# Two transformer blocks on one core: probabilities of the second block's attention turned by VectorE and DRAM instead of TensorE

## The chip, the cores and the metric

The kernel runs on one core of one Trainium2 chip. The metric is device time in microseconds (us). Three timed runs of the kernel before gave 1270.28, 1270.36 and 1270.67; their median is 1270.36.

## The reference

512 tokens of width 1024 in fp32 pass through two blocks. The first is a hybrid layer (a short convolution, stick-breaking attention, a state-space mixer and block attention, gated and merged, then a feed-forward layer). The second, in which the change lies, is this:

```python
h = rmsnorm_2(x, norm_g)
q, k, v, za, u, vs, zs, gm = jnp.split(h @ w_in, IN_SPLITS_2, axis=-1)
q = partial_rope(q.reshape(B, S, 16, 64), pos)     # 16 query heads of 64
k = partial_rope(k.reshape(B, S, 2, 64), pos)      # 2 key/value heads
a = window_sink_attention(q, k, v, att_sinks)      # below
a = (a * silu(za)) @ w_att_out
sgo = chunked_spatial_gating(gelu(u), gelu(vs), sg_w, sg_b, ln_g, ln_b)  # layer norm of vs, mixing weights sg_w
sgo = (sgo * silu(zs)) @ w_sg_out
ga, gs = jnp.split(sigmoid(gm + b_merge), 2, axis=-1)
x = rmsnorm_2(x + (ga * a + gs * sgo) @ w_o, final_g)

# window_sink_attention: chunks of 64 queries see their own chunk and the two before
s = einsum('bnqhgd,bnkhd->bhgnqk', qc, kb) * 64 ** -0.5
m = maximum(max(s), sink)
p = exp(s - m)
o = einsum('bhgnqk,bnkhd->bnqhgd', p / (sum(p) + exp(sink - m)), vb)
```

The value product sums over keys, so the probabilities, which come out of the softmax with a query in each partition, have to be turned until a key stands in each partition.

## The kernel before

**Matrix products.** A product with fp32 accuracy is made of three passes. Each weight tile that lands in `raw` is split in two: ScalarE makes the high part `whi` (`split`, line 1491), GpSimd the low part `wlo` as the rest (`rest`, lines 789 to 793). The activations stand in SBUF as `hh` and `hl`. TensorE then runs `whi` on `hh`, `whi` on `hl` and `wlo` on `hh` into one PSUM bank (`gemm_fm`, lines 961 to 969; `wide_unit`, lines 985 to 991, with tokens as the stationary side). Weights, high parts and low parts have two slots each. A unit is 256 columns of weights (1 MB); SyncE loads one when GpSimd has finished with its slot (`slot_free`), ScalarE splits it once TensorE has finished with the slot of its high part.

**The attention of the second block** is spread over these products. It has 32 steps s: 8 pairs of heads m, each with 4 token tiles c of 128 tokens. Two steps are a batch v (16 batches). The work of a batch is put into slots, small gaps that hooks open inside the products: in units of q and za after the k-th multiplication (table `W_AT`, six slots in a pair of units), then one slot behind each token tile of the four wide units (16 slots), then the rest at the first unit of the attention's output product. The same counter i runs over the slots on every engine:

- TensorE, `w_slot` (line 1360): in an even slot i the scores of batch i/2 (`w_scores`, line 1332) and the value products of steps i-4 and i-3 (`w_values`, line 1355); in every slot the transposes of step i-2 (`w_turn`, line 1343). The first token tile of a head pair sees 128 keys of its own only and takes two transposes and two value products; the other tiles see 256 and take four of each.
- VectorE: in an even slot the maximum over the scores (`w_soft`), then, after ScalarE's exponentials, the sums and the multiplication by the reciprocal (`w_norm`, lines 2690 to 2696). Once per head pair it multiplies the attention's output by the gate (`w_out`, semaphore `w_o`).
- ScalarE: exponentials in an even slot (`w_exp`, lines 1839 and 1843), and in each slot the copy of the turned tile from PSUM to `wpt` (`w_turned`, line 1852). Between them it makes the high parts of the weights.

The semaphores: `w_ps` scores made, `w_nm` maximum made, `w_read` and `w_e` exponentials made, `w_p` probabilities made (`wp`, three buffers by step), `w_t` transposed, `w_pt` copied to `wpt`, `w_v` value products made.

**SyncE's queue** is a program written in order: weights of each unit, the swapped rows of the rotary embedding (`swap_rotary`), and the rows of x, which VectorE turns in blocks of 32 x 32 (line 2758) and SyncE stores to DRAM in four pieces (`store_turned`, line 718). A wait in it holds back everything behind it.

**The first block's attention** already turns its probabilities so: VectorE in blocks of 32 x 32, SyncE stores `p_blocks` to `p_rows` in four pieces and loads them back as `p_t` (`turned_through`, lines 628 to 639).

Of the kernel before, what the change touches and what calls it, by code (L numbers as in the profile page):

```python
# [29 lines left out]
P = 128  # L30
KD = DM // P
TT = SEQ // P
# [61 lines left out]
def build_program(nc, par_xt, cst1, cst2a, w_in, w_branch, w_o, w_gu, w_down, w_in2, sg_w, sg_b, ln_g,  # L94
# [8 lines left out]
    with ctx:  # L103
# [122 lines left out]
        wpt = place("wpt", [P, 2, SEQ], Z0 + 92)  # L226
        att_t = place("att_t", [P, SEQ], Z0 + 96)
# [94 lines left out]
        STEPS = KD * TT  # L322

# [46 lines left out]
        xs_rows = nc.dram_tensor("xs_rows", (SEQ, BW), f32, kind="Internal").ap()  # L370
        p_rows = nc.dram_tensor("p_rows", (2, P, 1280), f32, kind="Internal").ap()
# [180 lines left out]
        def _(sp):  # L552
# [75 lines left out]
            def turned_through(i):  # L628

                sp.wait_ge(sem("p_turned"), i + 1)  # L630
                for f in range(4):
                    sp.dma_start(p_rows[i % 2].rearrange("(j a) (k c) -> a k j c", a=32, c=P)[:, :, :, 32 * f:32 * f + 32],
                                 p_blocks[32 * f:32 * f + 32, :].rearrange("a (k j b) -> a k j b", j=4, b=32)).then_inc(sem("p_stored"), 16)
                if 2 <= i < HEADS + 2:
                    sp.wait_ge(sem("mo_o"), i - 1)
                elif i >= HEADS + 2:
                    sp.wait_ge(sem("st_o"), i - HEADS - 1)
                sp.wait_ge(sem("p_stored"), 64 * (i + 1))
# [22 lines left out]
            for f, (n0, part, h0) in enumerate(ffn_units):  # L661
# [21 lines left out]
                sp.dma_start(lng[:, :], ln_g.partition_broadcast(P)).then_inc(sem("c2_in"), 16)  # L683
                stream(n0 + part + 2, 2, down_from(2 * UC))
                sp.wait_ge(sem("tile_free"), tiles_before(n0 + part))
                sp.dma_start(lnb[:, :], ln_b.partition_broadcast(P)).then_inc(sem("c2_in"), 16)
                sp.dma_start(bsb[:, :, :].rearrange("p g i -> p (g i)"), sg_b.partition_broadcast(P)).then_inc(sem("c2_in"), 16)
# [33 lines left out]
            for p in range(4):  # L721
                for j, c0 in enumerate((I2_Q, I2_ZA)):
                    n = n_qz + 2 * p + j
                    slot_free(n)
                    load(n, cols(w_in2, c0 + p * UC, UC))
                    if p == 0 and j == 1:
                        sp.wait_ge(sem("key_s"), 1)
                        for a, b in ((0, 8), (8, 0)):
                            for kv in range(2):
                                sp.dma_start(key_t[a:a + 8, kv, :], key_s[64 * kv + b:64 * kv + b + 8, :]).then_inc(sem("key_in"), 16)  # L730
# [2363 lines left out]
```

## Time and profile before

| | |
|---|---|
| median of three runs | 1270.36 us |
| the profiled execution | 1270.71 us |
| its span, first to last instruction | 1268.9 us |
| mean granted clock of TensorE | 0.999 |
| TensorE busy | 1261.5 us |
| VectorE busy | 893.3 us |
| GpSimd busy | 724.1 us |
| ScalarE busy | 619.7 us |

How to read it: the trace holds one execution, whose own time stands beside its span; what lies between the two, 1.8 us, is outside the recorded instructions. Busy times of an engine are sums over its instructions. Matmuls are pipelined: one starts before the last has ended, so the distance from start to start tells what an instruction adds to the stream, not its duration. Times in the rows below are us from the start of the span.

### The profile page before, as it was taken

To read this page: it belongs to the slowest core of one execution; us is meant where nothing else is said; L and a number is where in the kernel's file an instruction comes from. 1 tells how busy PE (TensorE), PEld (TensorE's weight loads), DVE (VectorE), ACT (ScalarE), POOL (GpSimd) and SP (SyncE) were. 2 spreads that over 40 slices of the span, in tenths; PEclk is the share of its full clock that TensorE was granted. 3 is DMA by queue.
4 is the path that set the end of the run, shared out by engine and by line. 5 is a ranking of instruction groups with operands and counts; after the bars stand their busy time and mean duration, and the time that the engine had idled before them with its cause. 6 is when DMAs were issued, how large, how long until landed. Compare 5 with 4: busy or idle time off the path is not lost.

```text
span 1268.9 us, 19753 instructions
## 1 busy us (share of the span) xinstructions
PE 1261.5 (99%) x7542; PEld 1091.2 (86%) x7542; DVE 893.3 (70%) x1380; ACT 619.7 (49%) x989; POOL 724.1 (57%) x513
## 2 busy tenths in 40 slices
PE   9999999999999999999999999999999999999998
PEld 7877877777888899989988998877778899999886
DVE  6775555777444599558855869766656999998587
ACT  6123533565334555325522546354556656666454
POOL 3543433434543588658865866444333786666767
PEclk9999999999999999999999999999999999999999
DMA  7253176564423335353535335333522233225351
GB/s 225 87 150 108 42 199 159 144 187 125 124 75 100 100 100 166 100 166 100 167 101 166 103 106 174 108 88 88 137 67 68 76 121 100 89 83 199 100 210 73
DMA packets 205371, 154.89 MB, mean 122 GB/s; under 512 B 67488, under 2 KB 194976, under 8 KB 204512
## 3 DMA queue, kind: packets, MB, share of 16 engines
q1 hardware_dynamic: 204800, 153.06, 40.3%
q8 instruction: 60, 0.98, 0.3%
q10 hardware_dynamic: 480, 0.59, 0.1%
q14 instruction: 31, 0.25, 0.1%
HBM read 136.20 MB, written 14.16 MB: 118 GB/s over the span
## 4 chain that ended last, share of the span: by engine, by line
PE 96%; ACT 1%; DVE 1%; DMA 1%; POOL 1%; issue 0%; SPq 0%; ACTq 0%
PE gemm L961 16%; PE gemm L962 16%; PE gemm L969 16%; PE gemm L1235 10%; PE gemm L1234 10%; PE gemm L1239 10%; PE gemm L985 2%; PE gemm L986 2%; PE gemm L991 2%; PE gemm L1018 2%; PE gemm L1019 2%; PE gemm L1024 2%; PE mix L1355 1%; PE mix L1343 1%; PE mix L1332 1%; DMA raw<-w_in 1%
## 5 line engine op out<-in xcount | busy, mean ns | idle before, releaser
L793 POOL TENSOR_TENSOR wlo<-raw,whi 128x512 fp32r<-128x512 f32 x264 | 368.7, 1428 | 288.6 <-ACT whi L1491 269.1
L961 PE MATMUL gemm<-hh,whi 128*128 128x512 f32 x544 | 215.3, 396 | 0.2 <-ACT whi L1491 0.2
L962 PE MATMUL gemm<-hl,whi 128*128 128x512 f32 x544 | 212.4, 390 | 0.0
L813 POOL TENSOR_TENSOR wlo<-raw,whi 128x512 fp32r<-128x512 f32 x108 | 159.4, 1501 | 40.5 <-ACT whi L1685 32.4
L1491 ACT ACTIVATE whi<-raw 128x2048 fp32r<-128x2048 f32 x62 | 118.4, 1909 | 46.0 <-PE gemm L969 19.8
L969 PE MATMUL gemm<-hh,wlo 128*128 128x512 f32 x544 | 136.0, 391 | 0.0
L1234 PE MATMUL gemm<-hh,whi 128*128 128x256 f32 x496 | 124.8, 284 | 0.0
L961 PEld LDWEIGHTS gemm<-hh,whi 128*128 128x128 f32 x544 | 102.1, 188 | 26.3 <-issue 4.3
L1235 PE MATMUL gemm<-hl,whi 128*128 128x256 f32 x496 | 124.4, 284 | 0.0
L962 PEld LDWEIGHTS gemm<-hl,whi 128*128 128x128 f32 x544 | 102.3, 188 | 20.4
L969 PEld LDWEIGHTS gemm<-hh,wlo 128*128 128x128 f32 x544 | 101.7, 188 | 20.9
L789 POOL TENSOR_TENSOR wlo_b<-raw_b,whi_b 128x512 fp32r<-128x512 f32 x16 | 20.7, 1292 | 137.4 <-ACT whi L1491 137.4
L1235 PEld LDWEIGHTS gemm<-hl,whi 128*128 128x128 f32 x496 | 95.4, 192 | 0.2
L1234 PEld LDWEIGHTS gemm<-hh,whi 128*128 128x128 f32 x496 | 95.2, 192 | 0.4 <-DVE parts L2542 0.2
L1717 ACT ACTIVATE whi<-mix 128x512 fp32r<-128x512 f32 x92 | 54.7, 594 | 67.5 <-PE gemm L1239 42.3
L1235 PE MATMUL gemm<-t_lo,whi 128*128 128x256 f32 x320 | 80.3, 284 | 0.0
L1234 PE MATMUL gemm<-t_hi,whi 128*128 128x256 f32 x320 | 80.3, 284 | 0.0
L1239 PE MATMUL gemm<-hh,wlo 128*128 128x256 f32 x496 | 79.8, 284 | 0.0
L1239 PEld LDWEIGHTS gemm<-hh,wlo 128*128 128x128 f32 x496 | 68.5, 192 | 0.0
L2501 DVE TENSOR_TENSOR wlo<-mix,whi 128x512 fp32r<-128x512 f32 x92 | 62.8, 684 | 3.5 <-ACT whi L1717 3.1
L1508 ACT ACTIVATE gt<-gt 128x512 f32<-128x512 f32 x32 | 20.2, 631 | 91.0 <-DVE gt L2403 91.0
L1235 PEld LDWEIGHTS gemm<-t_lo,whi 128*128 128x128 f32 x320 | 61.6, 192 | 0.0
(545 smaller groups left out, 3124.6 us busy)
## 6 DMA issues: line engine op xcount, KB each, us to landing
raw<-w_in SPq DMA_DIRECT2D x53, 1024.0 KB, 5.3
raw<-w_gu SPq DMA_DIRECT2D x44, 512.0 KB, 5.2
raw<-w_down SPq DMA_DIRECT2D x16, 512.0 KB, 4.4
p_rows<-p_blocks SPq DMA_DIRECT2D x32, 160.0 KB, 3.2
p_t<-p_rows SPq DMA_DIRECT2D x8, 640.0 KB, 4.0
raw<-w_o SPq DMA_DIRECT2D x5, 1024.0 KB, 5.2
raw_b<-w_branch SPq DMA_DIRECT2D x16, 256.0 KB, 6.8
blk_b<-w_o SPq DMA_DIRECT2D x8, 512.0 KB, 7.1
```

The costliest lines, as they stand in the source:

```text
L793: last = nc.gpsimd.tensor_tensor(a(wlo), a(raw), as_f32(a(whi)), ALU.subtract)
L813: return nc.gpsimd.tensor_tensor(part_of(wlo, u, b), raw_block(u, f, k), as_f32(part_of(whi, u, b)), sub)
L961: mm(bank[:, :], w, xh[:, k, :], start=(k == 0), stop=False)
L962: mm(bank[:, :], w, xl[:, k, :], start=False, stop=False)
L969: last = mm(bank[:, :], wlo_[:, s, k, col:col + P], xh[:, k, :], start=False, stop=(k == kts - 1))
L985: mm(o, hh[:, 4 * half + i, tok], w, start=(half == 0 and i == 0), stop=False)
L1234: mm(o, wk, x(xi, k)[0], start=(k == 0), stop=False)
L1235: mm(o, wk, x(xi, k)[1], start=False, stop=False)
L1239: last = mm(o, part_of(wlo, u, b)[:, k, :], x(xi, k)[0], start=False, stop=(k == u.kt - 1))
L1491: fn(a(whi), a(raw), ACT.Copy).then_inc(sem("hi_done"), 1)
L1717: fn(part_of(whi, u, b), src, ACT.Copy).then_inc(sem("s_hi"), 1)
L2501: tt(part_of(wlo, u, b), sum_view(u, b), as_f32(part_of(whi, u, b)), ALU.subtract).then_inc(sem("s_lo"), 1)
```

## The change

For the first 12 of the 16 batches (`BY_DMA`, steps below `S_PE` = 24) the transposes on TensorE and ScalarE's copies to `wpt` are gone. In their place VectorE turns the probabilities of a batch in blocks of 32 x 32 into `w_blocks` (`w_blockwise`, behind `w_norm`; semaphore `w_tb`), SyncE stores them to `w_rows` in DRAM in four pieces of 128 KB (`store_probs`, `w_stored`) and loads them back with the blocks in their places (`load_probs`, 512 KB, `w_in`). TensorE's value products of these batches stand one slot later, in the odd slot 2v+5 instead of the even slot 2v+4, and read their moving operand in four runs of 32 columns. `w_blocks` and `w_turned_p` have two buffers each. Since these lie where the scale and shift of the layer norm (`lng`, `lnb`) and the bias of the mixing (`bsb`) are kept later, the loads of those three move behind the value products of step 23. The last 4 batches go as before.

SyncE's program for this part is written out in a new order, with the stores and loads of the probabilities between the weights and the rows of x. In ScalarE's program the high part of the next unit stands in front of the slots of a tile instead of behind them. In the first block, the stores of a head's probabilities stand behind the wait for the products of the head two before, instead of in front of it.

```diff
@@ -224,6 +224,8 @@
         wpt = place("wpt", [P, 2, SEQ], Z0 + 92)
+        w_blocks = [place(f"w_blocks{i}", [P, 1024], Z0 + at) for i, at in enumerate((80, 98))]
+        w_turned_p = [place(f"w_turned_p{i}", [P, 1024], Z0 + 68 + 4 * i) for i in range(2)]
@@ -320,6 +322,8 @@
         STEPS = KD * TT
+        BY_DMA = 12
+        S_PE = 2 * BY_DMA
@@ -368,6 +372,7 @@
         xs_rows = nc.dram_tensor("xs_rows", (SEQ, BW), f32, kind="Internal").ap()
+        w_rows = nc.dram_tensor("w_rows", (2, P, 1024), f32, kind="Internal").ap()
@@ -628,13 +633,13 @@
                 sp.wait_ge(sem("p_turned"), i + 1)
-                for f in range(4):
-                    sp.dma_start(p_rows[i % 2].rearrange("(j a) (k c) -> a k j c", a=32, c=P)[:, :, :, 32 * f:32 * f + 32],
-                                 p_blocks[32 * f:32 * f + 32, :].rearrange("a (k j b) -> a k j b", j=4, b=32)).then_inc(sem("p_stored"), 16)
+                for f in range(4):
+                    sp.dma_start(p_rows[i % 2].rearrange("(j a) (k c) -> a k j c", a=32, c=P)[:, :, :, 32 * f:32 * f + 32],
+                                 p_blocks[32 * f:32 * f + 32, :].rearrange("a (k j b) -> a k j b", j=4, b=32)).then_inc(sem("p_stored"), 16)
@@ -680,11 +685,7 @@
                 sp.dma_start(cs2[:, :, :], cst2a.rearrange("p (a s) -> p a s", a=2)).then_inc(sem("c2_in"), 16)
-                sp.dma_start(lng[:, :], ln_g.partition_broadcast(P)).then_inc(sem("c2_in"), 16)
-                sp.wait_ge(sem("tile_free"), tiles_before(n0 + part))
-                sp.dma_start(lnb[:, :], ln_b.partition_broadcast(P)).then_inc(sem("c2_in"), 16)
-                sp.dma_start(bsb[:, :, :].rearrange("p g i -> p (g i)"), sg_b.partition_broadcast(P)).then_inc(sem("c2_in"), 16)
@@ -718,33 +719,91 @@
                                  x_turned[m % 4][32 * f:32 * f + 32, :].rearrange("a (j b) -> a j b", b=32)).then_inc(sem("x_stored"), 16)
...
+            def store_probs(v):
+
+                sp.wait_ge(sem("w_tb"), v + 1)
+                if v >= 2:
+                    sp.wait_ge(sem("w_v"), 2 * v - 2)
+                for f in range(4):
+                    sp.dma_start(w_rows[v % 2].rearrange("(j a) c -> a j c", a=32)[:, :, 256 * f:256 * f + 256],
+                                 w_blocks[v % 2][32 * f:32 * f + 32, :].rearrange("a (j c) -> a j c", j=4)).then_inc(sem("w_stored"), 16)
+
+            def load_probs(v):
+
+                sp.wait_ge(sem("w_stored"), 64 * (v + 1))
+                sp.dma_start(w_turned_p[v % 2][:, :], w_rows[v % 2]).then_inc(sem("w_in"), 16)
+
+            def load_qz(n):
+                slot_free(n)
+                p, j = divmod(n - n_qz, 2)
+                load(n, cols(w_in2, (I2_ZA if j else I2_Q) + p * UC, UC))
+
...
+            load_qz(n_qz)
+            load_qz(n_qz + 1)
+            sp.wait_ge(sem("key_s"), 1)
+            for a, b in ((0, 8), (8, 0)):
+                for kv in range(2):
+                    sp.dma_start(key_t[a:a + 8, kv, :], key_s[64 * kv + b:64 * kv + b + 8, :]).then_inc(sem("key_in"), 16)
+            load_qz(n_qz + 2)
+            swap_rotary(0)
+            load_qz(n_qz + 3)
+            load_qz(n_qz + 4)
+            store_probs(0)
...
+            store_probs(9)
+            load_probs(9)
+            store_probs(10)
+            load_probs(10)
+            slot_free(n_ao)
+            load(n_ao, cols(w_ao, 0, UC))
+            store_probs(11)
+            load_probs(11)
+            sp.wait_ge(sem("w_v"), S_PE)
+            sp.dma_start(lng[:, :], ln_g.partition_broadcast(P)).then_inc(sem("c2_in"), 16)
+            sp.dma_start(lnb[:, :], ln_b.partition_broadcast(P)).then_inc(sem("c2_in"), 16)
+            sp.dma_start(bsb[:, :, :].rearrange("p g i -> p (g i)"), sg_b.partition_broadcast(P)).then_inc(sem("c2_in"), 16)
-                slot_free(n_vs + u)
-                load_wide(u)
-                store_turned(4 + u)
-            stream(n_ao, 4, both(tiles_of(w_ao, 0)))
+                slot_free(n_ao + u)
+                load(n_ao + u, cols(w_ao, u * UC, UC))
@@ -1336,8 +1395,8 @@
                 pe.wait_ge(sem("w_p"), s + 1)
-                if s >= 1:
-                    pe.wait_ge(sem("w_pt"), s)
+                if s > S_PE:
+                    pe.wait_ge(sem("w_pt"), s - S_PE)
@@ -1346,14 +1405,20 @@
                 m, c = s // TT, s % TT
-                pe.wait_ge(sem("w_pt"), s + 1)
+                if s < S_PE:
+                    pe.wait_ge(sem("w_in"), 16 * (s // 2 + 1))
+                    by_block = w_turned_p[s // 2 % 2].rearrange("p (f k b) -> p k f b", k=8, b=32)
+                    turned = lambda k: by_block[:, s % 2 * 4 + k]
+                else:
+                    pe.wait_ge(sem("w_pt"), s - S_PE + 1)
+                    turned = lambda k: wpt[:, s % 2, k * P:(k + 1) * P]
-                                  wpt[:, s % 2, (2 * h + kb_) * P:(2 * h + kb_ + 1) * P],
+                                  turned(2 * h + kb_),
@@ -1363,10 +1428,11 @@
                         w_scores(i // 2)
-                    for s in (i - 4, i - 3):
-                        if 0 <= s < STEPS:
-                            w_values(s)
-                if 0 <= i - 2 < STEPS:
+                first = i - 4 if i % 2 == 0 else i - 5
+                if (S_PE <= first < STEPS) if i % 2 == 0 else (0 <= first < S_PE):
+                    w_values(first)
+                    w_values(first + 1)
+                if S_PE <= i - 2 < STEPS:
@@ -1833,8 +1899,10 @@
                     s = 2 * v + e
-                    if s >= 3:
-                        act.wait_ge(sem("w_t"), s - 2)
+                    if s >= S_PE + 3:
+                        act.wait_ge(sem("w_t"), s - 2 - S_PE)
+                    elif s >= 3:
+                        act.wait_ge(sem("w_tb"), (s - 3) // 2 + 1)
@@ -1844,8 +1912,8 @@
             def w_turned(s):
-                act.wait_ge(sem("w_t"), s + 1)
-                if s >= 2:
+                act.wait_ge(sem("w_t"), s + 1 - S_PE)
+                if s >= S_PE + 2:
@@ -1861,7 +1929,7 @@
                 i = pos[0]
-                if 0 <= i - 2 < STEPS:
+                if S_PE <= i - 2 < STEPS:
@@ -1880,10 +1948,10 @@
                     for j in range(2):
+                        if j == 0 and p + u > 0:
+                            split(n + u + 1)
-                        if j == 0 and p + u > 0:
-                            split(n + u + 1)
@@ -2634,7 +2702,7 @@
             T = tiles_before(n_e0)
-            dve.wait_ge(sem("c2_in"), 64)
+            dve.wait_ge(sem("c2_in"), 16)
@@ -2656,6 +2724,8 @@
             def attention_consts():
+                for h in range(2):
+                    v.memset(w_blocks[0].rearrange("p (j k b) -> p k j b", j=4, b=32)[:, 2 * h], 0.0)
@@ -2696,6 +2766,21 @@
                     last.then_inc(sem("w_p"), 1)
+            def w_blockwise(v_):
+                dve.wait_ge(sem("w_p"), 2 * v_ + 2)
+                if v_ >= 2:
+                    dve.wait_ge(sem("w_stored"), 64 * (v_ - 1))
+                blocks = w_blocks[v_ % 2].rearrange("p (j k b) -> p k j b", j=4, b=32)
+                for s in (2 * v_, 2 * v_ + 1):
+                    probs = wp[:, s % 3].rearrange("p h (k j b) -> p (h k) j b", j=4, b=32)
+                    own = blocks[:, s % 2 * 4:s % 2 * 4 + 4]
+                    if s % TT == 0:
+                        for k in (1, 3):
+                            last = v.transpose(own[:, k], probs[:, k])
+                    else:
+                        last = v.transpose(own, probs)
+                last.then_inc(sem("w_tb"), 1)
+
@@ -2715,6 +2800,8 @@
                         w_norm(i // 2)
+                    if i < S_PE:
+                        w_blockwise(i // 2)
@@ -2819,6 +2906,7 @@
                 dve.wait_ge(sem("ln_rs"), 1)
+                dve.wait_ge(sem("c2_in"), 64)
```

On TensorE, before, the odd slot i = 5 of the first pair of units that has slots, which stands between two low products of a tile (`gemm`); `wp` are the probabilities, `c_58` the unit matrix of the transposes:

```order
L969 MATMUL gemm<-hh,wlo 128x512 [waits lo_done]
L969 MATMUL gemm<-hh,wlo 128x512 x3
L1343 MATMUL mix<-c_58,wp 128x128 [waits w_pt,w_p]
L1343 MATMUL mix<-c_58,wp 128x128 x3
L969 MATMUL gemm<-hh,wlo 128x512 x4
```

Four transposes stand there, of the second step of batch 1. TensorE after, the same slot; `v_159` are the values:

```order
L1028 MATMUL gemm<-hh,wlo 128x512 [waits lo_done]
L1028 MATMUL gemm<-hh,wlo 128x512 x3
L1420 MATMUL mix<-w_turned_p_164,v_159 64x128 [waits w_in]
L1420 MATMUL mix<-w_turned_p_164,v_159 64x128
L1420 MATMUL mix<-w_turned_p_164,v_159 64x128 [waits w_in]
L1420 MATMUL mix<-w_turned_p_164,v_159 64x128 x3
L1028 MATMUL gemm<-hh,wlo 128x512 x4
```

The transposes are gone; the slot now holds the value products of batch 0, which stood in the even slot before it and now wait for the load of the turned probabilities (`w_in`).

On VectorE, before, in the first pair of units that has slots, the scaling of a batch's probabilities (`wp`), the tile of za and the tiles of x:

```order
L2696 TENSOR_SCALAR wp<-wp,sml 128x128 [waits dve_link]
L2696 TENSOR_SCALAR wp<-wp,sml 128x128
L2696 TENSOR_SCALAR wp<-wp,sml 128x256 x2
L2101 SCALAR_TENSOR_TENSOR za<-gemm,R 128x512 [waits tile_done]
L2762 SCALAR_TENSOR_TENSOR prm_xT<-prm_xT,r_133 128x512 [waits tile_free]
L2758 STREAM_TRANSPOSE x_turned_138<-prm_xT 128x512 [waits x_scaled]
```

Nothing stands between the scaling and the tile of za. VectorE after:

```order
L2766 TENSOR_SCALAR wp<-wp,sml 128x128 [waits dve_link]
L2766 TENSOR_SCALAR wp<-wp,sml 128x128
L2766 TENSOR_SCALAR wp<-wp,sml 128x256 x2
L2779 STREAM_TRANSPOSE w_blocks_162<-wp 128x4x32 [waits w_stored,w_p]
L2779 STREAM_TRANSPOSE w_blocks_162<-wp 128x4x32
L2781 STREAM_TRANSPOSE w_blocks_162<-wp 128x4x4x32
L2169 SCALAR_TENSOR_TENSOR za<-gemm,R 128x512 [waits tile_done]
L2849 SCALAR_TENSOR_TENSOR prm_xT<-prm_xT,r_133 128x512 [waits tile_free]
L2845 STREAM_TRANSPOSE x_turned_138<-prm_xT 128x512 [waits x_scaled]
```

Three block transposes came in between: two of 128 columns for the first token tile, one of 512 for the second.

On SyncE, before, for the second and third pair of units, with weights (`raw`), rotary rows (`rope_t`) and rows of x (`x_rows`):

```order
L557 DMA raw<-w_in 128x8x256 [waits lo_done] x2
L711 DMA rope_t<-rope_s 8x1024 [waits tile_free]
L711 DMA rope_t<-rope_s 8x1024 x3
L718 DMA x_rows<-x_turned_136 32x16x32 [waits x_turned]
L718 DMA x_rows<-x_turned_136 32x16x32 x3
L557 DMA raw<-w_in 128x8x256 [waits lo_done]
L718 DMA x_rows<-x_turned_137 32x16x32 [waits x_stored,x_turned]
L718 DMA x_rows<-x_turned_137 32x16x32 x3
L557 DMA raw<-w_in 128x8x256 [waits lo_done]
```

Weights, rotary rows and rows of x alternate. SyncE after:

```order
L562 DMA raw<-w_in 128x8x256 [waits lo_done] x2
L728 DMA w_rows<-w_blocks_162 32x4x256 [waits w_tb]
L728 DMA w_rows<-w_blocks_162 32x4x256 x3
L712 DMA rope_t<-rope_s 8x1024 [waits tile_free]
L712 DMA rope_t<-rope_s 8x1024 x3
L734 DMA w_turned_p_164<-w_rows 128x1024 [waits w_stored]
L719 DMA x_rows<-x_turned_136 32x16x32 [waits x_turned]
L719 DMA x_rows<-x_turned_136 32x16x32 x3
L728 DMA w_rows<-w_blocks_163 32x4x256 [waits w_tb]
L728 DMA w_rows<-w_blocks_163 32x4x256 x3
L562 DMA raw<-w_in 128x8x256 [waits lo_done]
L734 DMA w_turned_p_165<-w_rows 128x1024 [waits w_stored]
```

The stores of batch 0 (`w_rows`) now stand behind two weight loads and in front of the rotary rows, its load (`w_turned_p`) behind these, and the stores of batch 1 in front of the next weights.

## Rows read from the trace of the kernel before

**Rows 1.** Page, part 1: busy us of each engine, share, instructions.
```profile
PE 1261.5 (99%) x7542; PEld 1091.2 (86%) x7542; DVE 893.3 (70%) x1380; ACT 619.7 (49%) x989; POOL 724.1 (57%) x513
```

**Rows 2.** Waits of TensorE, whole run: engine line waited for: us in total, times, longest.
```profile
PE gemm L1039 <- DVE warm L2114: 1.1, 1, 1.1
```

**Rows 3.** Timeline of TensorE, 904 to 928: start, us, engine, line, operation, operands, count.
```profile
909.61 1.07 PE L991 MATMUL gemm<-wlo,hh 128*128 128x512 f32 x4
910.52 0.60 PE L1343 MATMUL mix<-c,wp 128*128 128x128 f32 x4
910.87 0.47 PE L985 MATMUL gemm<-whi,hh 128*128 128x512 f32 x1
...
912.79 1.07 PE L991 MATMUL gemm<-wlo,hh 128*128 128x512 f32 x4
913.79 0.77 PE L1332 MATMUL mix<-k,q 64*64 64x64 f32 x16
914.50 0.93 PE L1355 MATMUL mix<-wpt,v 128*64 128x128 f32 x12
915.35 0.66 PE L1343 MATMUL mix<-c,wp 128*128 128x128 f32 x4
915.76 0.47 PE L985 MATMUL gemm<-whi,hh 128*128 128x512 f32 x1
...
923.76 0.44 PE L1343 MATMUL mix<-c,wp 128*128 128x128 f32 x2
923.95 0.48 PE L985 MATMUL gemm<-whi,hh 128*128 128x512 f32 x1
...
926.79 0.60 PE L1343 MATMUL mix<-c,wp 128*128 128x128 f32 x4
```

**Rows 4.** Windows: stretch, us, busy us by engine (count), clock, DMA share, GB/s.
```profile
860.40:890.30 29.90, 29.90 (x210) 23.64 (x209) 19.95 (x41) 14.86 (x44) 11.49 (x8) 1.00 0.36 93
890.30:906.00 15.70, 15.70 (x107) 12.41 (x109) 13.11 (x27) 8.92 (x20) 6.42 (x5) 1.00 0.63 160
906.00:922.30 16.30, 16.30 (x130) 12.77 (x126) 8.28 (x23) 9.36 (x28) 4.65 (x5) 1.00 0.47 114
```

**Rows 5.** Timeline of VectorE, 860 to 925; in brackets the wait before and its releaser.
```profile
869.95 0.70 DVE L2758 STREAM_TRANSPOSE x_turned<-prm_xT 128x512 f32<-128x512 f32 x1
...
880.66 0.16 DVE L2690 TENSOR_REDUCE sml<-sml 128x4 f32<-128x8 f32 x1 [2.82 <-ACT sml L1843]
...
900.56 0.16 DVE L2690 TENSOR_REDUCE sml<-sml 128x4 f32<-128x8 f32 x1 [1.37 <-ACT sml L1843]
...
900.97 2.05 DVE L2696 TENSOR_SCALAR wp<-wp,sml 128x128 f32<-128x128 f32 x4
...
910.62 0.16 DVE L2690 TENSOR_REDUCE sml<-sml 128x4 f32<-128x8 f32 x1 [2.65 <-ACT sml L1843]
...
911.03 1.14 DVE L2696 TENSOR_SCALAR wp<-wp,sml 128x256 f32<-128x256 f32 x4
...
918.65 0.16 DVE L2690 TENSOR_REDUCE sml<-sml 128x4 f32<-128x8 f32 x1 [2.81 <-ACT sml L1843]
...
919.06 1.01 DVE L2696 TENSOR_SCALAR wp<-wp,sml 128x128 f32<-128x128 f32 x4
```

**Rows 6.** SyncE's queue at 893 us, and DMA issues: count, KB each, us to landing.
```profile
893.06 2.02 SPq L718 DMA_DIRECT2D x_rows<-x_turned  x4
...
raw<-w_in SPq DMA_DIRECT2D x53, 1024.0 KB, 5.3
...
x_rows<-x_turned SPq DMA_DIRECT2D x32, 64.0 KB, 1.9
...
xdt<-xs_rows SPq DMA_DIRECT2D x1, 512.0 KB, 3.9
```

**Rows 7.** Waits of SyncE's queue, 150 to 335: us in total, times, longest.
```profile
SPq L638 <- DMA p_rows<-p_blocks: 15.2, 6, 2.6
SPq L639 <- DMA p_rows<-p_blocks: 6.2, 2, 3.7
```

More of the change, by code:

```diff
@@ L719, in store_turned @@
                                  x_turned[m % 4][32 * f:32 * f + 32, :].rearrange("a (j b) -> a j b", b=32)).then_inc(sem("x_stored"), 16)
[L721 to L730, printed above, removed]
-                    if p >= 1 and j == 0:
-                        swap_rotary(p - 1)
-                    if p >= 2:
-                        store_turned(2 * (p - 2) + j)
@@ L735, in _ @@
-            slot_free(n_vs)
+            def store_probs(v):
[8 more added lines that the diff above has]
+                sp.dma_start(w_turned_p[v % 2][:, :], w_rows[v % 2]).then_inc(sem("w_in"), 16)
@@ L736, in load_wide @@
+            def load_qz(n):
+                slot_free(n)
+                p, j = divmod(n - n_qz, 2)
+                load(n, cols(w_in2, (I2_ZA if j else I2_Q) + p * UC, UC))
             def load_wide(u):
+                slot_free(n_vs + u)
                 slot = raw[:, (n_vs + u) % 2].rearrange("p (k a) c -> p k (a c)", a=2)
                 load(n_vs + u, cols(w_in2, I2_VS + u // 2 * 512, 512, 4 * (u % 2), 4), slot)
+            load_qz(n_qz)
+            load_qz(n_qz + 1)
+            sp.wait_ge(sem("key_s"), 1)
@@ new lines, in _ @@
+            for a, b in ((0, 8), (8, 0)):
[6 more added lines that the diff above has]
+            store_probs(0)
+            swap_rotary(1)
+            load_probs(0)
+            store_turned(0)
+            store_probs(1)
+            load_qz(n_qz + 5)
+            load_probs(1)
@@ L740, in _ @@
+            store_turned(1)
+            store_probs(2)
+            load_qz(n_qz + 6)
+            load_probs(2)
+            store_probs(3)
+            load_probs(3)
+            swap_rotary(2)
+            store_turned(2)
+            store_probs(4)
+            load_qz(n_qz + 7)
+            load_probs(4)
+            store_turned(3)
+            store_probs(5)
             load_wide(0)
+            load_probs(5)
+            store_probs(6)
+            load_probs(6)
             swap_rotary(3)
+            load_wide(1)
@@ L742, in _ @@
             store_turned(4)
+            store_probs(7)
+            load_probs(7)
+            store_turned(5)
+            load_wide(2)
+            store_probs(8)
+            store_turned(6)
+            load_probs(8)
+            load_wide(3)
+            store_turned(7)
+            store_probs(9)
[6 more added lines that the diff above has]
+            load_probs(11)
```

## The prediction

> **What bounds the kernel now.** I read the page's engine totals first, then who TensorE waited for, then the attention stretch of the second block by its timeline. TensorE is busy for 1261.5 of 1268.9 us [rows 1], and the longest that its matmuls waited for another engine is 1.1 us, at the very start [rows 2]. So any instruction taken out of TensorE's stream should shorten the run by its own spacing, until an engine that is now hidden becomes late. VectorE is that engine: it is busy for 19.95 of 29.9 us between 860.4 and 890.3, and for 13.11 of 15.7 us between 890.3 and 906 [rows 4].
>
> The profiled execution took 1270.71 us (span 1268.9, and 1.8 around it), 0.35 above the median of the three timed runs, 1270.36. I sum against 1270.71 and take 0.35 off at the end.
>
> **The change part by part.**
>
> *TensorE's transposes go.* Steps 0 to 23 lose their transposes. Six of them are first token tiles with two transposes, six are third tiles with four, both behind scores in an even slot; twelve stand in odd slots, four each: 84 instructions. Their summed durations overlap, so I go by starts: two take 923.76 to 923.95, 0.19; four in an even slot 915.35 to 915.76, 0.41; four in an odd slot 910.52 to 910.87, 0.35 [rows 3]. That is 6 x 0.19 + 6 x 0.41 + 12 x 0.35 = 7.8 us.
>
> *The value products move from the even slot, behind the scores, to an odd slot by themselves.* The instructions stay (12 take 914.50 to 915.35, 0.85), but each of the twelve groups now follows a large matmul directly. Two rows show what that costs: behind four low products the transposes of an odd slot start after 0.91 (909.61 to 910.52), the scores after 1.00 (912.79 to 913.79) [rows 3]. The small ones that change the shape from the large ones most, as the scores do, pay 0.09 more; I charge the value products the same, 12 x 0.09 = 1.1, with bounds of 0, as the transposes, and twice 1.1. TensorE saves 7.8 - 1.1 = 6.7 us, 0.56 a batch, with bounds 5.6 and 7.8. The moving operand is now read in four pieces of 32 columns; no row shows such a read. If it doubled the 0.85, twelve groups would lose 10 us; if it is free, 0; I take 0, since the scores are read in pieces of 64 to 192 columns at the same pace, 0.71 for 16.
>
> A rule of the Trainium skill speaks against this exchange. The rows show a transpose spaced at 0.1 us on TensorE [rows 3] and a VectorE one of four times the width at 0.70 [rows 5]. "VectorE: DVE Perf Modes", section "The three transpose paths", gives TensorE 390 ns for a full 128 x 128 and VectorE 311 ns for one that is only done inside 32 x 32 blocks, and its rules send a full one to TensorE. By its 390 ns the removal would be worth an estimated 84 x 0.39 = 33 us. The spacing of the rows decides, since here the instructions are pipelined; the rule's advice ignores which engine is full.
>
> *VectorE gets the turning.* A pair of batches adds three transposes of 512 columns and two of 128. The first form takes 0.70 in the row of the x tiles [rows 5]; two small ones of 128 columns are bounded by the same row from above and by a quarter of it from below, 0.18, and I take 0.27. A pair costs 3 x 0.70 + 2 x 0.27 = 2.64 us, twelve batches 15.8. The output goes to strips of 32 columns, which no row shows: bounds are 2.64 and twice that. Is it hidden? Between 860.4 and 890.3 VectorE's 19.95 plus three batches, 3.96, makes 23.9; TensorE's stretch shrinks to 29.9 - 1.7 = 28.2. That leaves 4.3 for VectorE's waits on ScalarE's exponentials, of which the longest there is 2.82 [rows 4, 5]. It fits, with little over. Between 890.3 and 906 it does not: 13.11 + 1.5 x 1.32 + a wait of 1.37 = 16.5 against 15.7 - 0.85 = 14.9, a slip of 1.6. From 906 to 922.3: 8.28 + 2.65 + 2.81 + 2.64 = 16.4 against 15.2, a slip of 1.2, less what ScalarE wins by its lost copies of the transposed tiles. VectorE slips by up to 2.8 us.
>
> What waits for it: the scores of the next batch need the exponentials of the last one. Before, those of the batch at 906 had ended when VectorE went on at 910.62, and the next scores start at 913.79 [rows 3, 5]: 3.2 us of room. The slip nearly uses this up, and one more thing asks for VectorE: from an odd slot the value products of each new head pair need the gate product of the pair before, one slot earlier than they used to be free of it. I charge 1.0 us of stall around the last turned batches; the bounds are 0 and 2.8.
>
> *The path through DRAM.* Batch 9: its probabilities are ready at 911.03 + 1.14 = 912.2; two transposes 1.4, four store issues 2.0 (as the four of x rows), landing 1.9, the load of 512 KB 3.9 [rows 5, 6]: 921.4. The value products stand in the slot that began at 926.79 [rows 3]; two and a half batches' savings, 1.4, and the value products that leave the slot before, some 1.3, pull it to 924.1. The load has 2.7 us to spare. A weight load of 1 MB ahead of it takes 5.3 [rows 6] and could make it 2.6 late; the stores stand in front of the weights, so that a batch meets the weights once at most and usually while its stores are on the way. I take 0, bounds 0 and 2.6.
>
> *The rest of SyncE's queue.* Weight loads now stand behind waits for VectorE. The weight load behind the first stores comes some 3 us later, an estimate from four issues and the wait for the turning; what covers it is that ScalarE makes a unit's high parts while the unit before is still multiplied. Scale and shift of the layer norm and the mixing bias move behind the value products of step 23; they are needed only after the attention. Both cost 0; if the cover were gone, one late weight load would cost its 5.3 less that cover.
>
> *High parts in front of ScalarE's slots.* Same instructions, earlier; a slot behind a high part can wait for its weights, which have landed by then. 0. GpSimd's low parts come earlier with them and fall on other VectorE work: the multiply of four pieces takes 2.05 at 900.97, with GpSimd at work, and 1.01 at 919.06, without [rows 5]. The Trainium skill, "SBUF — State Buffer", section "Who interferes with whom", says that GpSimd and such a VectorE form lock each other out, and that a form with one SBUF input outside the fast modes does not. The trace agrees, 0.70 for a transpose at 869.95 inside GpSimd's work. What it makes of the time is in the second rival.
>
> *First block.* The stores of its probabilities now stand behind the wait that stood in front of the load. In the trace all eight loads there are released by their own stores, never by TensorE [rows 7]; the moved wait is over when it is reached. 0; else up to the 3 us of its stores per head.
>
> Sum: 1270.71 - 6.7 + 1.0 = 1265.0; less 0.35, **1264.7 us**.
>
> **The rivals.**
>
> *Nothing stalls.* ScalarE's lost copies shorten VectorE's waits enough, and the whole saving arrives: 1270.36 - 6.7 = 1263.7, or 1262.6 with the 7.8. For it: VectorE still waits 2.8 at a time for ScalarE. Against: 13.11 busy of 15.7 leaves no room.
>
> *VectorE or the queue paces the attention.* If the multiply collides with GpSimd in half of the twelve batches (6 x 1.0) or the load of probabilities comes 2.6 late in two of them, TensorE waits 3 to 6 us in all: 1270.36 - 6.7 + 4.5 = 1268.2, between 1266.7 and 1272. For it: the 2.05 row. Against: that collision cost TensorE nothing before.
>
> *Slower: block transposes at twice the price.* VectorE then gets 31.7 instead of 15.8 us. In each 28.2 us stretch it needs 4 more, more than the margin there; over three stretches and the wide units it slips by about 3 x 3 + 2.8 + 2 = 14, of which some 3.2 is room: TensorE stalls 10.5 and loses 10.5 - 6.7 = 3.8, **1274.2**. It decides from a slip of 6.7 + 3.2 = 10 us, 0.8 a batch over what I charge. Against: a stream of 32 x 32 blocks should not care where a block goes, but that is not shown.
>
> **How the numbers follow.** The likeliest case, 1263.5 to 1267, gets 0.52; no stall 0.17; a paced attention 0.20; slower 0.11. A measurement of this kernel tells about 0.2%, 2.5 us, from no change, so faster means below 1267.8: 0.52 + 0.17 + 0.06 = 0.75; the same is 0.14, the rest of the paced case; slower, above 1272.9, 0.11. The range is 1262.4 to 1270.8: it holds the first two cases and most of the third, and leaves out the slower one and the tails.
>
> **What would show it.** Right: TensorE's line of the transposes has 28 records instead of 112; the stretch from the first scores to the last value products is 5 to 7 us shorter; TensorE's waits name VectorE or ScalarE at the scores around the last turned batches, with about a us. The new transposes should read 0.70 for 128x4x4x32. Wrong: a transpose of 1.4 (slower); waits for the DMA of the probabilities at many value products, or value groups of 1.7 instead of 0.85. Anything lost outside the attention stretch would be a part that I counted as free.

## The result and the profile after

The changed kernel takes 1275.2 us, median of six runs (1274.28 to 1276.73), against 1270.43 before: a ratio of 1.0037 with an interval of 1.0027 to 1.0047, slower by 4.8 us where 1264.7 was forecast. The profiled execution took 1275.3 us.

The page's first part and TensorE's waits of the changed kernel (engine, line waited for: us, times, longest) answer to [rows 1] and [rows 2]:

```profile
PE 1257.1 (99%) x7458; PEld 1083.2 (85%) x7458; DVE 918.2 (72%) x1412; ACT 607.6 (48%) x959; POOL 729.4 (57%) x513
```
```profile
PE mix L1391 <- ACT wp L1907: 5.0, 4, 2.9
PE mix L1420 <- DVE att_t L2786: 2.8, 2, 1.8
PE gemm L1098 <- DVE warm L2182: 1.1, 1, 1.1
PE mix L1420 <- DMA w_turned_p<-w_rows: 1.1, 1, 1.1
PE mix L1402 <- DVE wp L2766: 0.2, 1, 0.2
```

84 matmuls are gone, as counted. But TensorE, which had waited for nothing in the attention, now waits 9.1 us there: 5.0 for exponentials, 2.8 for the gate product on VectorE, 1.1 for a load of turned probabilities, 0.2 for scaled ones. VectorE is busy 24.9 us longer, not the 15.8 that were charged.

All of the loss lies in the attention: the scores of batch 14 start at 946.34 before and at 950.96 after, 4.6 later, and that stays. The same stretch, from the first scores to those of batch 14, in both kernels (columns as in [rows 4]), before:

```profile
818.80:946.34 127.54, 127.54 (x892) 100.31 (x891) 81.25 (x180) 67.48 (x195) 48.49 (x36) 1.00 0.38 100
```

and after, with VectorE's waits in it:

```profile
818.50:950.96 132.46, 123.42 (x808) 92.44 (x807) 105.66 (x210) 52.81 (x163) 53.34 (x36) 0.99 0.68 190
```
```profile
DVE sml L2760 <- ACT sml L1911: 24.2, 14, 2.4
```

After, VectorE is busy 105.7 us and waits 24.2 for ScalarE's exponentials, 129.9 of 132.5: nothing is free. Before, its waits in that stretch were these:

```profile
DVE sml L2690 <- ACT sml L1843: 25.9, 14, 2.8
DVE sml L2684 <- PE mix L1332: 7.3, 5, 2.8
DVE sml L2682 <- PE mix L1332: 4.9, 3, 2.5
```

The first line is the one to read. 25.9 us of VectorE's idle time were a wait in the middle of each batch, with the sums and the scaling next in its order, so that work put behind the scaling cannot use it; and it hardly shrank when VectorE ran late (24.2). 127.5 - 81.3 - 25.9 leaves 20.4 us, of which 12.2 are the waits for scores in the other two lines. TensorE's saving shortens the stretch by 6, to 14.4; the change asks for 24.4. The missing 10 us are TensorE's waits, and a stretch at half clock behind the longest of them. This balance says how much is missing over the whole stretch, and not where or why; the experiments below show that a sum which fits is not enough.

VectorE's groups in the attention (line, form, count, busy us, mean ns), before:

```profile
L2728 DVE SCALAR_TENSOR_TENSOR za<-za_e,za 128x512 f32<-128x512 f32 x6 | 3.9, 684 | 0.0
L2705 DVE TENSOR_TENSOR atl<-att_t,ath 128x512 fp32r<-128x512 f32 x5 | 3.4, 685 | 0.0
```

and after:

```profile
L2781 DVE STREAM_TRANSPOSE w_blocks<-wp 128x512 f32<-128x512 f32 x18 | 11.9, 684 | 0.2
L2815 DVE SCALAR_TENSOR_TENSOR za<-za_e,za 128x512 f32<-128x512 f32 x6 | 8.6, 1472 | 0.0
L2790 DVE TENSOR_TENSOR atl<-att_t,ath 128x512 fp32r<-128x512 f32 x5 | 5.5, 1093 | 0.0
L2815 DVE SCALAR_TENSOR_TENSOR za_last<-za_e,za_last 128x512 f32<-128x512 f32 x2 | 3.5, 1769 | 0.0
L2779 DVE STREAM_TRANSPOSE w_blocks<-wp 128x128 f32<-128x128 f32 x12 | 3.0, 291 | 0.2
```

The block transposes cost 11.9 + 3.0 = 14.9 us, near the 15.8 charged. The rest of the 24.4, 9.5 us, is old work that became slower: the products that prepare the gates went from 684 to 1472 ns. One pair of them, 3.47 us where it took 1.28 before (at 862.70), comes ahead of TensorE's first wait:

```profile
864.28 3.47 DVE L2815 SCALAR_TENSOR_TENSOR za<-za_e,za 128x512 f32<-128x512 f32 x2
...
874.16 0.78 PE L1391 MATMUL mix<-k,q 64*64 64x64 f32 x16 [1.28 <-ACT wp L1907]
```

A later pair stands, behind the turning of its batch, in front of a gate product that TensorE waits for; on VectorE after (start, us):

```profile
894.85 1.30 DVE L2781 STREAM_TRANSPOSE w_blocks<-wp 128x512 f32<-128x512 f32 x2
896.08 2.56 DVE L2815 SCALAR_TENSOR_TENSOR za<-za_e,za 128x512 f32<-128x512 f32 x2
898.68 0.69 DVE L2786 TENSOR_TENSOR att_t<-mix,za 128x512 f32<-128x512 f32 x1
```

GpSimd makes low parts at that time:

```profile
895.11 6.89 POOL L852 TENSOR_TENSOR wlo<-raw,whi 128x512 fp32r<-128x512 f32 x4 [9.06 <-ACT whi L1557]
```

The Trainium skill, "SBUF — State Buffer", section "Who interferes with whom", says that VectorE's operations with two inputs in SBUF contend with a GpSimd instruction that reads SBUF; the pair above, 1.28 us each instead of 0.68, agrees. The gate product `att_t` ends at 899.37 and TensorE's value products start at 899.51, after a wait of 1.85.

The longest wait, on TensorE after, in answer to [rows 3]:

```profile
907.42 1.08 PE L1050 MATMUL gemm<-wlo,hh 128*128 128x512 f32 x4
908.43 1.15 PE L1420 MATMUL mix<-w_turned_p,v 128*64 128x128 f32 x16
...
915.42 0.77 PE L1391 MATMUL mix<-k,q 64*64 64x64 f32 x16 [2.86 <-ACT wp L1907]
...
917.41 0.63 PE L1044 MATMUL gemm<-whi,hh 128*128 128x512 f32 x1
917.84 0.63 PE L1045 MATMUL gemm<-whi,hl 128*128 128x512 f32 x1
...
920.67 0.93 PE L1420 MATMUL mix<-w_turned_p,v 128*64 128x128 f32 x12
921.52 0.50 PE L1044 MATMUL gemm<-whi,hh 128*128 128x512 f32 x1
```

and two windows of it (granted clock in the third column from the end):

```profile
912.50:915.40 2.90, 0.06 (x1) 0.00 (x0) 0.87 (x2) 1.96 (x9) 0.77 (x1) 1.00 1.09 267
917.00:920.40 3.40, 3.40 (x10) 2.66 (x8) 3.29 (x8) 1.14 (x3) 0.00 (x0) 0.52 0.99 312
```

After 2.9 idle us the large matmuls start 0.43 apart (917.41 to 917.84) instead of 0.23 (922.56 to 922.79 in the same trace) for 3.4 us, at a granted clock of 0.52, the 1.2 GHz level: another 1.5 us.

### The profile page after: what moved, and what is told of

The parts are those of the page before. It is cut to its first block and busy times, and to the rows that moved or that the text cites. A ratio compares the mean times of both kernels' runs of the same rounds, so it can differ in the third digit from the quotient of the medians.

```text
span 1273.5 us, 19610 instructions
## 1 busy us (share of the span) xinstructions
PE 1257.1 (99%) x7458; PEld 1083.2 (85%) x7458; DVE 918.2 (72%) x1412; ACT 607.6 (48%) x959; POOL 729.4 (57%) x513
## 5 line engine op out<-in xcount | busy, mean ns | idle before, releaser
L852 POOL TENSOR_TENSOR wlo<-raw,whi 128x512 fp32r<-128x512 f32 x264 | 374.1, 1448 | 287.8 <-ACT whi L1557 268.3
L872 POOL TENSOR_TENSOR wlo<-raw,whi 128x512 fp32r<-128x512 f32 x108 | 159.4, 1501 | 40.6 <-ACT whi L1751 32.5
L1293 PEld LDWEIGHTS gemm<-t_hi,whi 128*128 128x128 f32 x320 | 61.4, 192 | 0.0
```

The source lines that it names most:

```text
L852: last = nc.gpsimd.tensor_tensor(a(wlo), a(raw), as_f32(a(whi)), ALU.subtract)
L872: return nc.gpsimd.tensor_tensor(part_of(wlo, u, b), raw_block(u, f, k), as_f32(part_of(whi, u, b)), sub)
L1293: mm(o, wk, x(xi, k)[0], start=(k == 0), stop=False)
```

## The experiments

Times are medians; "before" ran beside each.

**High parts behind the slots again** (the changed kernel, ScalarE's order undone).

```diff
-                        if j == 0 and p + u > 0:
-                            split(n + u + 1)
                         for _ in W_AT[2 * u + j] if p else ():
                             w_slot()
+                        if j == 0 and p + u > 0:
+                            split(n + u + 1)
```

> The changed kernel with one part undone: in ScalarE's program the high part of the next unit stands behind the slots of a tile again, as before. Theory A (collisions): in the changed kernel's attention stretch VectorE was busy 105.6 us against 81.2 before, 24.4 more, of which the block transposes are 14.9 and some 9.5 are two-input operations of VectorE that became slower beside GpSimd's low parts (the gate products of za 684 ns before, 1472 ns after); the early high parts cause it. It expects VectorE's busy time in that stretch to fall by 6 to 9 us, TensorE's waits to fall from 9 us to under 3, and 1265 to 1268 us. Theory B (the turning alone fills VectorE, whatever GpSimd does): 1274 to 1276 us, within 1 us of the changed kernel's 1275.2, with 8 us of waits or more. Theory C (the path through DRAM and SyncE's new order hold TensorE up): no change either, with waits named after the load of the probabilities.

Measured: 1274.15 us, ratio 1.0029 (1.0018 to 1.0041). TensorE's new wait there:

```profile
PE gemm L1050 <- POOL wlo L852: 3.2, 1, 3.2
```

Theory A's 1265 to 1268 did not come: VectorE's busy time in the stretch fell by 0.9 us, to 104.5, and the gate preparations still took 1249 ns. The time and TensorE's 8.8 us of waits are those of theory B. With the order undone low parts once come 3.2 us late, yet the kernel is not slower for it.

**Only the high parts moved** (the kernel before with the reverse of that edit).

> The kernel before with this one part of the change done: the high part of the next unit stands in front of ScalarE's slots. Theory A: the collisions appear here too, without any turning: the gate products of za take over 1.2 us each instead of 0.68 and VectorE is busy 5 us or more longer between the first scores and the last turned batch; VectorE has some 20 us free there, so the time stays within 1.5 us of 1270.4. Theory B says nothing on it. If the gate products stay at 0.68 us, the collisions come from VectorE running late and not from the early high parts, and theory A has the wrong cause.

Measured: 1270.33 against 1270.53, ratio 0.9998 (0.9989 to 1.0008), and

```profile
L2728 DVE SCALAR_TENSOR_TENSOR za<-za_e,za 128x512 f32<-128x512 f32 x6 | 3.9, 685 | 0.0
```

So the early high parts cost nothing by themselves and cause no collisions in the kernel before: theory A has the wrong cause. Its expectation then lays the collisions on VectorE running late. That was not tested here, and *No turning, rows late* below speaks against it for most of them.

**No turning** (the changed kernel without the block transposes).

```diff
...
-                    if s % TT == 0:
-                        for k in (1, 3):
-                            last = v.transpose(own[:, k], probs[:, k])
-                    else:
-                        last = v.transpose(own, probs)
+                if v_ < 2:
+                    last = v.memset(w_blocks[v_][:, :], 0.0)
+                else:
+                    last = v.transpose(w_blocks[v_ % 2][:, 0:32], wp[:, (2 * v_ + 1) % 3, 0, 128:160])
```

> The changed kernel with VectorE's turning left out: in place of three block transposes a pair, VectorE makes one of 32 columns per batch (so the attention's output is not the reference's); the stores, loads, waits and value products stay. Theories A and B: TensorE's saving shows, 1263 to 1266 us, with waits under 2 us. Theory C (the path holds TensorE up): the waits for the load of the probabilities and for ScalarE stay, 1271 us or more.

Measured: 1270.07 us, ratio 0.9999 (0.9989 to 1.0008), in none of the three ranges: TensorE's waits for VectorE and ScalarE are gone, and waits for the load, theory C's sign, have come in their place. TensorE was 4.9 us ahead of before at the scores of batch 10 (908.87 against 913.79) and then waited for two loads, the first of them here, with SyncE's queue ahead of it:

```profile
914.41 0.93 PE L1420 MATMUL mix<-w_turned_p,v 128*64 128x128 f32 x12 [1.82 <-DMA w_turned_p<-w_rows]
...
925.74 0.45 PE L1420 MATMUL mix<-w_turned_p,v 128*64 128x128 f32 x4 [3.69 <-DMA w_turned_p<-w_rows]
```
```profile
903.36 2.47 SPq L728 DMA_DIRECT2D w_rows<-w_blocks  x4
905.92 3.39 SPq L719 DMA_DIRECT2D x_rows<-x_turned  x4
910.37 0.34 SPq L734 DMA_DIRECT2D w_turned_p<-w_rows  x1
```

The path through DRAM is a second limit, hidden in the changed kernel behind VectorE: four stores of x rows, 3.39 us of issue, stand here between a batch's stores and its load. At the second load four more (4.87 us of issue from 911.98) stand in front of the batch's own stores.

**Turning only** (TensorE still transposes; nobody reads the blocks).

```diff
-        S_PE = 2 * BY_DMA
+        S_PE = 0
-                    if i < S_PE:
+                    if i < 2 * BY_DMA:
                         w_blockwise(i // 2)
```

All stores and loads of probabilities, and the waits for them, are taken out too, and the high parts stand as before.

> The changed kernel with only the turning on VectorE: TensorE still transposes for all batches and takes its values from there, the block transposes of 12 batches go to a buffer that nobody reads, no stores and loads; the high parts stand behind ScalarE's slots as before. It prices the turning alone. VectorE had 127.4 us in the stretch before, 81.2 busy and 25.9 waiting for ScalarE's exponentials, so some 20 us free, against 15 us of turning. Theory A: TensorE waits under 2 us and the time is 1270 to 1272 us. Theory B: 4 us of waits or more, 1274 us or more.

Measured: 1275.69 us, ratio 1.0046 (1.0031 to 1.0061): theory B, though with 2.9 us of waits and not 4. TensorE's wait and the clock behind it:

```profile
PE mix L1396 <- DVE att_t L2760: 2.9, 2, 2.5
```
```profile
914.60:917.00 2.40, 0.00 (x0) 0.00 (x0) 2.37 (x6) 0.08 (x1) 0.00 (x0) 1.00 1.16 308
918.90:921.40 2.50, 2.50 (x7) 1.97 (x6) 0.07 (x1) 2.39 (x11) 0.00 (x0) 0.50 0.00 0
```

The turning alone makes the kernel 5.2 us slower, without any path through DRAM. By the sum over the stretch it should have fitted: 20.4 us were free, the turning takes 14.9 and old work became 2.8 us slower (99.0 us busy). Nor did it cost a little in every batch: the scores of batch 10 start at 913.76, against 913.79 before, and those of batch 11 at 926.00, against 921.87. Nearly all of it is lost in between. Before, VectorE's gate product there was

```profile
912.09 0.68 DVE L2701 TENSOR_TENSOR att_t<-mix,za 128x512 f32<-128x512 f32 x1
```

and with the turning VectorE and TensorE read

```profile
913.42 0.16 DVE L2736 TENSOR_REDUCE sml<-sml 128x4 f32<-128x8 f32 x1 [2.37 <-ACT sml L1887]
...
915.00 1.31 DVE L2755 STREAM_TRANSPOSE w_blocks<-wp 128x512 f32<-128x512 f32 x2
916.23 0.65 DVE L2760 TENSOR_TENSOR att_t<-mix,za 128x512 f32<-128x512 f32 x1
...
917.03 0.90 PE L1396 MATMUL mix<-wpt,v 128*64 128x128 f32 x12 [2.49 <-DVE att_t L2760]
```

VectorE goes on behind the exponentials at 913.42, 2.8 us later than before (910.62 in [rows 5]): the turning of the batch before took 1.0, and three old instructions around it took 2.2 longer beside GpSimd's low parts. Then it turns, 1.31 us, in front of the gate product. That product ends at 916.88 instead of 912.77. TensorE's value products, which started at 914.50 before [rows 3], had 1.7 us of room.

**Six batches** (`BY_DMA = 6`, and the other six stores and loads removed).

> The changed kernel with 6 turned batches in place of 12: batches 6 to 11 stay on TensorE's transposes, their stores and loads are gone. In the changed kernel TensorE's scores of batch 5 stood 2.6 us earlier than before and it had waited for nothing until then. Theory B (VectorE's turning uses up its free time after some six batches): half of the saving arrives, 1267 to 1268.5 us, with under 1 us of waits in the stretch. If the turning costs from the first batch on, or the early high parts do, 1270 us or more.

Measured: 1271.11 us (1269.44 to 1273.10), ratio 1.0008 (0.9998 to 1.0017): theory B's 1267 to 1268.5 was a miss, and the time is that of the other case. But the turning does not cost from the first batch on either: in the profiled execution TensorE was 2.5 us ahead at the scores of batch 5 (863.31) and then waited 0.5 and 1.9 by 885.5, for exponentials and for scaled probabilities. Half a turning behind the scaling doesn't pay. Why the runs spread over 3.7 us one trace doesn't tell.

**Rows of x late** (the changed kernel; `store_turned(4)` to `(7)` behind `load_probs(11)`).

> The changed kernel with the last four stores of x rows moved behind the last load of probabilities in SyncE's queue. Where only VectorE holds TensorE up, 1274.5 to 1276 us. Where the queue is half of it (without turning, TensorE still waited 5.5 us for two loads of probabilities, and both loads were issued behind a store of x rows), the waits for the load of the probabilities go and the time falls by 1 to 2 us at most, since VectorE's waits stay: 1273 to 1274.5 us.

Measured: 1275.37 us, ratio 1.0038 (1.0024 to 1.0053). The wait for the load is gone; those for exponentials and the gate product are 7.8 us, as in the changed kernel (5.0 + 2.8), and the time did not fall. So the path through DRAM decides nothing as long as VectorE is late.

**No turning, rows late** (the two edits together).

> VectorE's turning left out as in the third experiment (so the attention's output is not the reference's), and the last four stores of x rows behind the last load of probabilities. If the order of the queue made those loads late: waits for them under 1 us, no stretch at half clock, and TensorE's saving shows whole, 1264 to 1266 us. If the DMA engines are full whatever the order (0.97 to 0.99 busy around the first of those waits): waits of 3 us or more remain and 1268 us or more.

Measured: 1264.62 us, ratio 0.9954 (0.9937 to 0.9970), with one wait of 1.7 us for a load in the slowest, profiled execution. The order of the queue had made the loads late, and TensorE's saving is 5.8 us. VectorE's stretch in this run, to the scores of batch 14, and its gate preparations there:

```profile
818.50:941.57 123.07, 121.33 (x807) 91.24 (x806) 92.85 (x191) 53.88 (x164) 53.64 (x36) 1.00 0.69 197
L2808 DVE SCALAR_TENSOR_TENSOR za<-za_e,za 128x512 f32<-128x512 f32 x6 | 8.1, 1394 | 0.0
```

VectorE is busy 92.9 us against 81.3 before. 3.9 of that are the small block transposes and the two fills that stand in for the turning; the rest, over 7 us, is old work that is slower beside GpSimd, although next to nothing is turned and TensorE never waits for VectorE in the attention. So most of the changed kernel's 9.5 us of slower work do not come from VectorE being late, and by themselves they cost TensorE nothing. The high parts alone do not bring them either; which other part of the change does was not tested.

**Turning in the wait** (a new order). The turning with `i // 2 - 1` stands between `w_soft` and `w_norm`; `OUT_AT` are the slots of the gate product; the value products of batches 4 to 10 move to slot 2v+6.

```diff
-        BY_DMA = 12
+        BY_DMA = 11
+        OUT_AT = (7, 11, 17, 21, 25, 27, 31, 35)
...
+                if i % 2 == 0 and 4 <= i // 2 - 1 < BY_DMA:
+                    w_blockwise(i // 2 - 1)
...
                 if i % 2 == 0:
                     if i < STEPS:
                         w_norm(i // 2)
-                    if i < S_PE:
+                    if i < 8:
                         w_blockwise(i // 2)
```

> A new order of the changed kernel's work: from batch 4 on VectorE turns a batch's probabilities while it waits for ScalarE's exponentials of the next batch (it waits 24 us there in the changed kernel, some 2.4 us a batch, against 1.3 us of turning); the value products of these batches stand one slot later, 11 batches are turned instead of 12, and SyncE's queue has weights ahead of stores and two stores of x rows at the end. If VectorE was late because the turning stood where it could not use that wait: VectorE's wait for the exponentials falls to about 12 us, TensorE waits under 2 us, 1264.5 to 1267 us. If VectorE's sum of work is the limit, or the path through DRAM, 1270 us or more, with waits for ScalarE's exponentials or for the load of the probabilities.

Measured: 1266.82 us, ratio 0.9973 (0.9963 to 0.9984): 3.6 us faster than before. TensorE still waited 3.2 us, all for the gate product. VectorE's wait for exponentials fell to 19.7 us up to the scores of batch 14, not to 12: the batches outside 5 to 11 wait as ever.

**The same with the turning behind the scaling** (that move alone undone).

> The eighth experiment (11 batches, value products one slot later, the new order of SyncE's queue; 1266.82 us) with one thing undone: VectorE turns a batch right behind its scaling again, as in the changed kernel. If the place of the turning is what won 8 us against the changed kernel, VectorE's wait for the exponentials stays at 24 us or more and TensorE's waits come back: 1271 us or more. If the later value products and the new queue order won it, 1268 us or less.

Measured: 1276.48 us, ratio 1.0046 (1.0029 to 1.0063), with VectorE's wait for exponentials at 25.8 us and

```profile
PE mix L1419 <- DVE att_t L2790: 6.1, 4, 2.2
PE mix L1390 <- ACT wp L1909: 3.7, 4, 1.4
```

The later value products and the new queue win nothing by themselves; the place of the turning is worth 9.7 us. That includes slower old work that comes and goes with it: VectorE is busy 103.7 us here to the scores of batch 14, and 97.8 with the turning in the wait.

**The gate product in the wait too.**

```diff
                     w_blockwise(i // 2 - 1)
+                if i + 1 in OUT_AT[2:5]:
+                    w_out(OUT_AT.index(i + 1))
...
```

> The eighth experiment with VectorE's gate product of head pairs 2 to 4 moved into the wait for the exponentials too, one slot earlier. TensorE's last three waits there (3.2 us) were all for this product. If VectorE's order is the limit: two of the three waits go, 1264.5 to 1266 us. If VectorE is simply late by its sum of work, other waits take their place, 1266 to 1268 us.

Measured: 1264.33 us (1263.64 to 1264.85), ratio 0.9953 (0.9937 to 0.9970): 6.1 us faster than before and 10.9 faster than the changed kernel. All three waits are gone, not two; TensorE waits for nothing in the attention. On VectorE a batch now reads

```profile
909.17 1.31 DVE L2783 STREAM_TRANSPOSE w_blocks<-wp 128x512 f32<-128x512 f32 x2
910.40 0.65 DVE L2790 TENSOR_TENSOR att_t<-mix,za 128x512 f32<-128x512 f32 x1
911.94 0.16 DVE L2762 TENSOR_REDUCE sml<-sml 128x4 f32<-128x8 f32 x1 [0.88 <-ACT sml L1913]
```

and its stretch to the scores of batch 14

```profile
818.80:939.16 120.36, 120.29 (x816) 92.62 (x815) 94.21 (x206) 54.73 (x166) 52.40 (x37) 1.00 0.72 203
```

94.2 busy us are the 81.3 of before and 13.5 of turning (16 and 12 transposes, 10.5 + 3.0): in this order VectorE's old work is in sum no slower than it was.

## Why the prediction was wrong

*TensorE's saving* was right: 6.7 forecast, with bounds of 5.6 and 7.8; 5.8 with nothing of VectorE in its way (no turning, rows late). The value products start 1.01 after four low products (907.42 to 908.43), 0.10 more than the transposes did where 0.09 was charged, and reading in strips of 32 columns is free: 12 take 0.85 (920.67 to 921.52), as in [rows 3]. The 390 ns that the prediction quotes from the Trainium skill ("VectorE: DVE Perf Modes", section "The three transpose paths") stand there for bf16, and these transposes are fp32. The 33 us that it estimates by them did not come; the 5.8 agree with the spacing of the rows.

*The price of a block transpose* was right, 14.9 us for 15.8, so the slower rival (twice the price, 1274.2) named a time near the measured one for a reason that did not happen.

*"I charge 1.0 us of stall around the last turned batches"*, with a bound of 2.8, is the step that failed: it became 9.1 us of waits and 1.5 at half clock. The charge set how late VectorE gets against the room that TensorE has, and both were wrong.

The room was read from one path only, the exponentials, 3.2 us. The gate product was named and not priced. It had 1.7 us of room, and the turning was put right in front of it. Turning only shows what that is worth: VectorE was 2.8 us late at batch 9, a slip of the forecast size though mostly for another reason, the gate product came 4.1 us late with the batch's own turning, and the kernel lost 5.2 us. Moving the turning alone, from behind the scaling into the wait, wins 9.7; moving the gate products too ends TensorE's waits.

The lateness was summed from VectorE's old work at its old price. In the changed kernel that work took 9.5 us more, which the sum had at nothing and left to a rival. *"It fits, with little over"* had no margin for it: the waits for exponentials between 860.4 and 890.3 were 0.39, 0.99 and 2.82 before, 4.2 of the 4.3 us that were left. The pair of gate preparations at 864.28, 2.2 us slower, falls into that stretch, and TensorE's first wait comes at 874.16, long before the last turned batches. The slower work alone is not enough either: with no turning and the rows late that pair takes 3.48 us, and TensorE never waits for VectorE.

The rival that VectorE or the queue paces the attention had the mechanism. Its price of 3 to 6 was too small, and gives 1266.7 to 1269.7, not the 1272 that stands as its end. It saw the collision in the multiply by the reciprocal; it was mostly in the gate preparations. What brings these together with GpSimd's low parts stays open.

*The path through DRAM*, charged 0 with a bound of 2.6 for a weight load in front, was a second error: stores of x rows, not weights, held the loads up, and it cost 5.5 us of waits once VectorE was out of the way. In the changed kernel it decides nothing.

*The high parts' new place*, charged 0, is confirmed at 0 by itself. The first block's moved wait and the late constants have no experiment of their own; the scores of batch 0 start at 818.57 instead of 818.89, and outside the attention TensorE has no new wait over 0.2 us.

## What to carry to other kernels

Idle time of an engine that works in order is free only for what stands in front of its wait. Before giving an engine work, split its idle time by what ended it, add all the waits of a kind, and put the new work into the wait itself. A sum that fits is not enough: list everything that another engine waits for behind the new work, and price the one with the least room. Where two limits lie behind each other, take each away alone: here either one ate the whole saving.

## What the runs showed of the hardware

A wait of 2.5 us (turning only) or 2.9 us (the changed kernel) on TensorE was followed by some 3 us at a granted clock of 0.50 to 0.52, which cost some 1.5 us more; the wait of 3.2 us with the high parts behind the slots left it at 1.00, so that it does not follow each time:

```profile
900.00:903.50 3.50, 0.35 (x2) 0.00 (x0) 3.18 (x6) 3.04 (x6) 3.50 (x4) 1.00 0.40 92
903.50:908.00 4.50, 4.47 (x31) 3.31 (x32) 4.47 (x8) 0.00 (x0) 4.50 (x4) 1.00 1.03 264
```

The second window, behind the wait, stands at the full 2.4 GHz.
